# Relu and head sum of the late index scores, one head of up to 1024 keys at a time instead of two heads of up to 512

## The reference, cut to what matters

```python
def indexer_scores(q_idx, w_idx, k_idx, valid):
    dots = jnp.einsum("bqhd,bld->bqhl", q_idx, k_idx, preferred_element_type=jnp.float32) * (IDX_DIM ** -0.5)
    s = jnp.einsum("bqh,bqhl->bql", w_idx.astype(jnp.float32) * (N_IDX_HEADS ** -0.5), jax.nn.relu(dots))
    return jnp.where(valid, s, -jnp.inf)
```

## Time and profile before

| what | value |
|---|---|
| median of three runs | 2569.94 us |
| the profiled execution: its own time | 2576.68 us |
| the profiled execution: span, first to last instruction | 2574.9 us |
| mean granted TensorE clock | 0.868 of full speed |
| busy TensorE matmul, VectorE, ScalarE | 2195.9, 1408.6, 1177.4 us |
| relus L1081 | 224 instructions, 116.8 us |
| sums L1157 and L1153 | 196 and 28 instructions, L1157 136.0 us |

### The profile page before, as it was taken

How to read it: one execution, slowest core, us unless ns; L and a number is a source line. 1 busy time by engine, 2 the same in 40 slices (tenths; PEclk the granted TensorE clock), 3 DMA queues, 4 the chain that set the end, 5 groups by cost and what they waited for, 6 DMA issues and landing times.

```text
span 2574.9 us, 33463 instructions
## 1 busy us (share of the span) xinstructions
PE 2195.9 (85%) x12592; PEld 1728.9 (67%) x12592; DVE 1408.6 (55%) x3246; ACT 1177.4 (46%) x2401; POOL 134.0 (5%) x174
## 2 busy tenths in 40 slices
PE   7999899989968888898888888888878788897864
PEld 4777767667746666676676666666667668677762
DVE  2336767668421111145587777778786842434580
ACT  1112567676601122242375756667677658333000
POOL 0000000000000000000000000000000010101004
PEclk9999999999967788888898979888998889888556
DMA  7122122111123111121010110101010110114001
GB/s 267 67 82 69 65 76 69 64 65 58 57 75 115 45 46 46 61 63 56 11 58 26 35 52 11 50 11 50 11 33 11 33 44 9 44 66 140 1 1 34
DMA packets 60161, 140.05 MB, mean 54 GB/s; under 512 B 14096, under 2 KB 28344, under 8 KB 58976
## 3 DMA queue, kind: packets, MB, share of 16 engines
q1 hardware_dynamic: 57824, 127.43, 14.8%
q0 software_dynamic: 2176, 10.49, 1.2%
HBM read 97.92 MB, written 39.98 MB: 54 GB/s over the span
## 4 chain that ended last, share of the span: by engine, by line
PE 59%; DVE 15%; ACT 14%; issue 6%; DMA 4%; SPq 1%; POOL 1%; PEld 1%; DVEq 0%; POOLq 0%; ACTq 0%
PE psum L802 10%; PE psum L1381 8%; PE psum L1350 8%; PE psum L841 7%; PE psum L1392 7%; PE psum L1373 5%; ACT sb_lowj L283 4%; PE psum L1363 4%; PE psum L1339 2%; ACT sb_ptb L1055 2%; DVE sb_junk L1171 2%; DVE sb_sc L1157 2%; ACT sb_elow L283 2%; DMA sb_x<-in_x_prompt 1%; DMA sb_qa<-qt_s 1%
## 5 line engine op out<-in xcount | busy, mean ns | idle before, releaser
L1381 PE MATMUL psum<-sb_v,sb_ptb 128*128 128x64 f32 x2176 | 314.6, 290 | 32.3 <-ACT sb_ptb L1055 31.7
L802 PE MATMUL psum<-sb_w,sb_xt 128*128 128x512 f32 (+5 forms) x1088 | 335.7, 464 | 0.5 <-DVE sb_xt L538 0.5
L1381 PEld LDWEIGHTS psum<-sb_v,sb_ptb 128*128 128x128 f32 x2176 | 298.7, 211 | 51.3 <-ACT sb_ptb L1055 50.6
L1055 ACT ACTIVATE sb_ptb<-psum 128x512 f32<-128x512 f32 (+3 forms) x352 | 187.0, 534 | 225.4 <-PE psum L1373 224.9
L1373 PE MATMUL psum<-sb_con,sb_p 128*128 128x128 f32 x1280 | 234.7, 311 | 48.6 <-ACT sb_p L1111 27.3
L1350 PEld LDWEIGHTS psum<-sb_qa,sb_w 128*128 128x128 f32 x2048 | 247.8, 196 | 38.4 <-issue 26.0
L1350 PE MATMUL psum<-sb_qa,sb_w 128*128 128x128 f32 x2048 | 251.4, 280 | 25.7 <-DMA sb_w<-in_w_in 24.5
L1392 PE MATMUL psum<-sb_wo,sb_mix 128*128 128x512 f32 x512 | 256.2, 664 | 13.4 <-DVEq L1307 13.4
L802 PEld LDWEIGHTS psum<-sb_w,sb_xt 128*128 128x128 f32 (+1 forms) x1088 | 181.5, 187 | 126.7 <-issue 114.2
L841 PE MATMUL psum<-sb_xt,sb_w 128*128 128x128 f32 x2048 | 237.3, 275 | 0.0
L1363 PE MATMUL psum<-sb_ks,sb_qa 128*128 128x512 f32 (+3 forms) x640 | 190.3, 434 | 54.8 <-DMA sb_qa<-qt_s 31.2
(11 more groups left out here) (395 smaller groups left out, 2658.3 us busy)
## 6 DMA issues: line engine op xcount, KB each, us to landing
qt_s<-sb_qt SPq DMA_DIRECT2D x32, 512.0 KB, 3.0
sb_x<-in_x_prompt SPq DMA_DIRECT2D x16, 512.0 KB, 4.8
xt_s<-sb_xt SPq DMA_DIRECT2D x16, 512.0 KB, 2.6
sb_qa<-xt_s SPq DMA_DIRECT2D x16, 512.0 KB, 3.2
sb_qa<-qt_s SPq DMA_DIRECT2D x16, 512.0 KB, 3.5
sb_qa<-qt_s SPq DMA_DIRECT2D x32, 256.0 KB, 4.8
sb_xres<-in_x_prompt SPq DMA_DIRECT2D x16, 512.0 KB, 4.8
out_y_prompt<-sb_y SPq DMA_DIRECT2D x16, 512.0 KB, 3.0
```

What stands on the lines that cost most here:

```text
L802: mm = pe.matmul(out, m.xt[:, p, k, 0:n], m.w1[:, k, lo:hi], start=(k == 0), stop=(k == KD - 1))
L1055: act.activation(m.ptb[:, g, 0:cols], m.turn[slot][:, 0:cols], ACT.Copy).then_inc(s.t_act, 1)
L1381: mm = pe.matmul(o, m.ptb[:, g, x * P:(x + 1) * P], v, start=st, stop=sp)
```

## The change

The relu and the sum handle one head of up to 1024 keys. So a score slot holds one head of two banks instead of two heads of one bank each, and `m.r` has two places of 1024 instead of 512. The chunks of a tile are 1024 and the rest (128 to 1024), instead of three or four of up to 512. Every tile now has 16 slot uses, 16 relus and 16 sums; before, tiles 8 to 11 had 12 uses and 24 relus and sums, tiles 12 to 15 had 16 uses and 32. The matmuls stay the same in size and number, and their order is now by head. The search keeps its number of operations: a chunk wider than 512 carries six of ScalarE's (after heads 0 to 5) and two bits of VectorE's (at heads 0 and 3), a narrower one three and one.

```diff
 def plan():
-            for c in chunks(width(i + 1), 512):
-                scores += [(("D", i + 1, c, hp), "relu") for hp in range(4)]
+            for c in chunks(width(i + 1), 1024):
+                scores += [(("D", i + 1, c, h), "relu") for h in range(NIH)]
...
 def b_act(act, m, s):
-            for c in chunks(width(i + 1), 512):
-                for hp in range(4):
-                    slot, n, _, count = scores.of[("D", i + 1, c, hp)]
+            for c in chunks(width(i + 1), 1024):
+                for h in range(NIH):
+                    slot, n, _, count = scores.of[("D", i + 1, c, h)]
                     act.wait_ge(s.s_done, n)
-                    for e in range(2):
-                        if 2 * count + e > 3:
-                            act.wait_ge(s.acc, 2 * count + e - 3)
-                        act.activation(m.r[:, e, 0:c[1]], m.score(slot)[:, e, 0:c[1]], ACT.Relu).then_inc(s.relu, 1)
-                    if hp < 3:
+                    if count > 2:
+                        act.wait_ge(s.acc, count - 2)
+                    act.activation(m.r[:, h % 2, 0:c[1]], m.score2(slot)[:, 0:c[1]], ACT.Relu).then_inc(s.relu, 1)
+                    if h < (6 if c[1] > 512 else 3):
                         q = refine(u, q)
...
     def accumulate(i, c, h):
-        num = 2 * (scores.of[("D", i, c, h // 2)][3] - 1) + h % 2 + 1
+        num = scores.of[("D", i, c, h)][3]
...
 (b_vector, the steps)
-            for c in chunks(width(i + 1), 512):
-                if indexed(i):
-                    search(i, done, c, 0)
+            for c in chunks(width(i + 1), 1024):
+                h = 0
+                while indexed(i) and h < (6 if c[1] > 512 else 3):
+                    search(i, done, c, h)
                     done += 1
-                for h in range(3 if indexed(i) else 0, NIH):
+                    h += 3
+                for h in range(h, NIH):
                     accumulate(i + 1, c, h)
...
 def b_tensor(pe, m, s):
-            pe.wait_ge(frees[free[0]], free[1] * (2 if free[0] == "relu" else 1))
+            pe.wait_ge(frees[free[0]], free[1])
...
-    def index_pair(i, c, hp):
-        slot = slot_of(scores, ("D", i, c, hp))
-        for e in range(2):
+    def index_head(i, c, h):
+        slot = slot_of(scores, ("D", i, c, h))
+        for lo, n in chunks(c[1], 512):
             for x in range(2):
-                mm = pe.matmul(m.score(slot)[:, e, 0:c[1]], m.qi[:, x, 2 * hp + e, :], m.ks[:, 0, c[0]:c[0] + c[1]],
+                mm = pe.matmul(m.score2(slot)[:, lo:lo + n], m.qi[:, x, h, :], m.ks[:, 0, c[0] + lo:c[0] + lo + n],
                                start=(x == 0), stop=(x == 1))
         mm.then_inc(s.s_done, 1)
...
 program
-            m.r = sb(b, "r", [P, 2, 512])
+            m.r = sb(b, "r", [P, 2, 1024])
```

More of the change, by code:

```diff
@@ L1241, in b_vector @@
         if indexed(i + 1):
-            for c in chunks(width(i + 1), 512):
-                if indexed(i):
-                    search(i, done, c, 0)
+            for c in chunks(width(i + 1), 1024):
+                h = 0
+                while indexed(i) and h < (6 if c[1] > 512 else 3):
+                    search(i, done, c, h)
                     done += 1
-                for h in range(3 if indexed(i) else 0, NIH):
+                    h += 3
+                for h in range(h, NIH):
                     accumulate(i + 1, c, h)
-            dve.wait_ge(s.acc, 2 * scores.of[("D", i + 1, c, NIH // 2 - 1)][3])
+            dve.wait_ge(s.acc, scores.of[("D", i + 1, c, NIH - 1)][3])
         elif indexed(i):
@@ L1397, in b_tensor @@
         j = i - 2
-        pairs = [(c, hp) for c in chunks(width(i + 1), 512) for hp in range(4)] if indexed(i + 1) else []
+        pairs = [(c, h) for c in chunks(width(i + 1), 1024) for h in range(NIH)] if indexed(i + 1) else []
         if pairs:
@@ L1402, in b_tensor @@
             if n < len(pairs):
-                index_pair(i + 1, *pairs[n])
+                index_head(i + 1, *pairs[n])
                 if n == len(pairs) - 1:
```

## The result

The changed kernel takes 2548.47 us (median of 4 runs, 2545.78 to 2556.45), the kernel before beside it 2574.56 (4 runs, 2567.52 to 2587.29): a ratio of 0.9898 with a 95% interval of 0.985 to 0.9946. The forecast was 2546. The profiled execution has a span of 2554.6 us at a mean granted clock of 0.875.

The account below looks back on a forecast made before the run. TensorE was taken to lead tiles 8 to 11 and wait for VectorE's sums in the fronts of tiles 12 to 15, VectorE to lead their tails; 16.1 + 8.7 - 0.8 = 24.0 us less, 2546 us, range 2538 to 2562.

Parts of the forecast that it names:

- The fronts: Index parts of tiles 12 to 15 up to the ninth pair or head: fourth head needs no sum, 16.1 us less.
- tile 15: Front of tile 15: head 5 after 3.1 us idle, ninth head at 1869.4 instead of 1873.93, 4.5 us less.
- the half clock: Tile 15's front: slow TensorE clock after the wait before head 5, taken as 1.3 us, between nothing and 2.5.
- The tails: Index parts of tiles 12 to 15 after the front: eight sums instead of sixteen each, together 8.7 us less.
- The stall before the second sum of the last chunk: VectorE in the tails of tiles 12 to 15: a wait of about 1.2 us for a relu.
- the trains: Runs of six VectorE sums in the earlier profile, giving 0.33 us for each operation and 1.04 ns a key.
- Tiles 8 to 11: Index parts of these tiles, led by TensorE: 0.2 us more a tile, 0.8 in all.
- The rival "slower": Second chunks: wide pieces no longer overlap, from 0.39 us a head; 25 us slower, 2595 us; chance 0.07.
- the two rivals in which fronts or tails give nothing: Tiles 12 to 15: no gain in tails, 2555 us, chance 0.15; no gain in fronts, 2562 us, chance 0.10.
- Everything behind L1416 is carried along.: Work after the index part moves with its end, so a us taken from the index part leaves the step.
- The chain of the first section: Chain of work that ended last: ScalarE's search, begun again behind L1416, sets VectorE's `select` and the next first sum.

Follow-up runs that it names:

- F7: The changed kernel with the attention scores of the first head's first chunk computed twice in all sixteen steps; 2525.72 us, ratio 0.9787.
- F5: The changed kernel with four relu places of 1024 keys and the first head's first-chunk attention scores computed twice in the eight index steps; 2531.21 us, ratio 0.9805.
- F6: The changed kernel with the first head's first-chunk attention scores computed twice in the eight steps with an index part; 2531.34 us, ratio 0.9806.
- F1: The changed kernel with eight unneeded matmuls of 512 columns ahead of the memory score in steps with index work; 2553.38 us, ratio 0.9895.

## Why the prediction was right

**The fronts: right mechanism, 12.3 us of 16.1.** Heads 3 and 4 needed no sum, head 5 was the first to wait, and it came 1.92 us behind the first sum where I had 1.8. Tiles 12, 13 and 14 gave 4.5, 4.5 and 2.1 us for 4.7, 4.7 and 2.2. Waits before head 5 were 1.13, 1.84 and none for 0.8, 1.8 and none. The one term that missed is tile 15: 1.3 for 4.5 us. Two of its inputs were off. I had kept the first sum where it was against the first head's matmuls, 12.67 us behind (1855.07 - 1842.40); it came 14.36 us behind (wait 4.87 us, not 3.1). And for the half clock I had taken 1.3 us, between nothing and 2.5; four matmuls and a gate block took 0.9 and 1.7 us more than at full clock, 2.6 together. 1.7, 1.3 and the 0.1 of the hand-off make the 3.2 us that were missing. TensorE came to this index part 1.1 us sooner after the memory maximum (rest of tile 14 74.03 us, before 75.13), and the first sum did not: the gain turned into a longer wait, which F7's trace shows the other way round. With room for four heads the front took 22.81 us.

**The tails: 9.8 us, forecast 8.7.** That is 0.31 us for each of 32 sums; the trains had given 0.33. Tiles 12 to 15 gave 2.6, 2.8, 2.2 and 2.3 us. The stall before the second sum of the last chunk was 0.95 to 1.60 us, forecast about 1.2. VectorE led the tails, as forecast, and is busy 8.0 us less in them; the experiment without look-ahead kept the sum of these tails when the fronts' gain was gone. Look-ahead alone also shortened the tails by 4.6 us, a route that I had not considered; the two do not add up. The Trainium skill (Perfetto Trace Analysis, Optimizing Scalar/DVE Operations) has some 60 ns of overhead for a VectorE operation on SBUF, and about twice that in profiled latency. By these figures the tails would have given an estimated 2 to 4 us. This case's trace does not agree: 9.8 us.

**Tiles 8 to 11: level,** 0.3 us more for 0.8, and no narrow chunk shows slower hand-offs. The rival "slower" needed 0.39 us a head and is out; so are the two rivals in which fronts or tails give nothing.

**The sum: near 24.0 in part by luck.** These three terms, up to L1416, give 21.9 us of the forecast 24.0. The stretch up to the memory maximum gives 23.7 because another 1.9 us, which the forecast had left out, came behind L1416 in tiles 10 and 11. TensorE, before and after, tile 10:

```profile
1310.04 2.08 PE L1416 MATMUL psum<-sb_mkt,sb_qm 64*128 64x256 f32 x8 [3.15 <-ACT sb_gate L1098]
```

```profile
1313.95 1.13 PE L1417 MATMUL psum<-sb_mkt,sb_qm 64*128 64x256 f32 x8 [1.95 <-ACT sb_gate L1097]
```

The wait ahead of the memory score is shorter and the eight matmuls run at the full clock.

**"Everything behind L1416 is carried along."** This step carried the forecast, and it is only half shown. For this change the evidence agrees with it: between the two second traces 23.8 us came out of the index stretches and the rests were level, and both comparisons of medians, 26.1 us (2574.56 - 2548.47) and 29.3 (2577.95 - 2548.69), are no smaller than the forecast 24.0. But the spans of the two pairs of traces differ by only 20.3 and 17.4 us, and the rests were level only in their sum. The look-ahead at 512, and twice the four places, took 22, 13 and 12 us out of the same stretch and lost 12, 10 and 9 of it in the rests. The chain of the first section names engines, not their clock, and the matmuls of the rests take 57 or 49 us for the same work by what the clock is. Whether the lower clock in those kernels is a consequence of their earlier index parts, or the chance between executions, one trace of each cannot tell; that F5 and F6, and the four places and the change, have equal medians over six runs each speaks for a consequence, without showing it. What makes it so stays open. That the medians moved 2 to 5 us more than the forecast stays open as well; two executions of one kernel differ in the same code by 10 us, more than that.

## What to carry to other kernels

When a producer's wait is ended by a relu whose buffer waits for a slow consumer, look first at how many items the buffer holds: the wider buffer moved the wait one head back, and its 3.91 us became 1.13. Undo the halves of a change one at a time, since "bigger pieces" hid two gains here, room to run ahead and fewer operations; with the first undone the trace kept the second. Before trusting a gain on one stretch, compare two executions of the same kernel stretch by stretch: what repeats to 0.1 us and what wanders by 10 us are different kinds of evidence. And when TensorE comes out of a wait at half clock, repeat matmuls that it needs anyway, in a gap that another engine's work ends, not ahead of a point others wait for.

## What the hardware showed that I had not expected

- The same code took more or less time from one trace to the next, in whole blocks at a lower granted clock. The rest of tile 8 took 57.47 us at 0.77 and 52.17 at 0.87 in the two traces of the kernel before, and 49.49 at 0.96 in F1; that of tile 9 67.61 at 0.73 and 62.70 at 0.80, and 61.06 at 0.84 in the changed kernel. The eight rests of the changed kernel, though, repeated within 0.1 us.
- A wait of 1.84 us left four matmuls at 1.21 us, one of 3.88 us doubled them to 2.07, and the engine stayed at half clock through the gate block behind them (3.62 us for 1.95).
- Matmuls whose result nobody needs were worth 0.9% (F6) and 1.1% (F7) of the kernel's time by the ratios, where they cost no time of their own; put in ahead of the memory score, where they ran at half clock (3.75 us for 2.08), they were worth nothing (F1).
